# Running sums of a state-space scan: GpSimd multiplies the triangle, TensorE adds down with 512-column f32r products

## What is computed

```python
a = -jnp.exp(a_log)                       # one number for each head
a_cum = jnp.cumsum(dtc * a, axis=2)       # running sums down the 128 tokens of a chunk
seg = a_cum[:, :, :, None] - a_cum[:, :, None, :]
decay = jnp.exp(jnp.where(causal, seg, -jnp.inf))
cb = jnp.einsum('bctgn,bcsgn->bctsg', cc, bc)
y_diag = jnp.einsum('bctsgh,bcsghp->bctghp', cb[..., None] * decay, xdt)
```

## Time and profile before

| what | value |
|---|---|
| median of three runs | 1853.76 us (1853.33 to 1853.78) |
| the profiled execution | 1853.41 us |
| its span, first to last instruction | 1851.6 us |
| mean granted TensorE clock | 0.997 of full speed |
| TensorE busy | 1837.6 us, 99% |
| VectorE busy | 1293.0 us, 70% |
| ScalarE busy | 1024.6 us, 55% |
| GpSimd busy | 0.6 us |
| HBM traffic | 330.23 MB moved, mean 178 GB/s |

### The profile page before, as it was taken

The page is one execution under the profiler, slowest core; times in us unless marked ns, Lnnn a source line. Parts: engine busy times, 40 slices in busy tenths (PEclk is TensorE's granted clock), DMA queues, the critical chain, the costliest instruction groups (busy, mean ns, idle before and its releaser), DMA issues.

```text
span 1851.6 us, 27958 instructions
## 1 busy us (share of the span) xinstructions
PE 1837.6 (99%) x11450; PEld 1649.6 (89%) x11450; DVE 1293.0 (70%) x1775; ACT 1024.6 (55%) x1182; POOL 0.6 (0%) x7
## 2 busy tenths in 40 slices
PE   8999999999999999999999999999999999999998
PEld 8898889998889888899988888899988888889997
DVE  6868887986686887798656555677656555578654
ACT  6657745655465684465545456465544456556543
POOL 0000000000000000000000000000000000000000
PEclk9999999999999999999999999999999999999999
DMA  9776656655675765655555566465555556555553
GB/s 244 166 146 151 173 181 192 193 184 188 159 171 144 164 164 177 204 182 182 175 195 185 165 195 199 164 204 183 182 185 186 167 184 203 171 175 183 184 179 102
DMA packets 253319, 330.23 MB, mean 178 GB/s; under 512 B 25796, under 2 KB 165328, under 8 KB 253192
## 3 DMA queue, kind: packets, MB, share of 16 engines
q1 hardware_dynamic: 252928, 328.10, 58.9%
q10 hardware_dynamic: 264, 0.35, 0.1%
HBM read 327.33 MB, written 1.09 MB: 177 GB/s over the span
## 4 chain that ended last, share of the span: by engine, by line
PE 96%; DVE 2%; ACT 1%; DVEq 1%; DMA 0%; issue 0%; SPq 0%; ACTq 0%
PE psum L575 31%; PE psum L587 16%; PE psum L589 15%; PE psum L588 15%; PE psum L651 5%; PE psum L678 4%; PE psum L653 2%; PE psum L772 1%; PE psum L710 1%; DVEq L1413 1%; DMA w_raw<-in_w_in 0%; PE psum L791 0%; PE psum L918 0%; PE psum L955 0%; PE psum L935 0%; PE psum L598 0%
## 5 line engine op out<-in xcount | busy, mean ns | idle before, releaser
L400 ACT ACTIVATE w_hi<-w_raw 128x2048 fp32r<-128x2048 f32 (+2 forms) x310 | 575.7, 1858 | 312.9 <-PE psum L589 281.1
L575 PE MATMUL psum<-act,w_hi 128*128 128x256 f32 x3264 | 591.7, 284 | 0.0
L392 DVE TENSOR_TENSOR w_low<-w_raw,w_hi 128x1024 fp32r<-128x1024 f32 (+1 forms) x310 | 372.7, 1202 | 285.7 <-ACT w_hi L400 277.0
L575 PEld LDWEIGHTS psum<-act,w_hi 128*128 128x128 f32 x3264 | 510.2, 192 | 1.2 <-issue 0.7
L587 PE MATMUL psum<-w_hi,act 128*128 128x512 f32 x1280 | 505.1, 395 | 0.0
L589 PE MATMUL psum<-w_hi,act 128*128 128x512 f32 x1280 | 498.9, 390 | 0.0
L588 PE MATMUL psum<-w_low,act 128*128 128x512 f32 x1280 | 498.5, 389 | 0.0
L575 PE MATMUL psum<-act,w_low 128*128 128x256 f32 x1632 | 462.5, 283 | 0.0
L393 DVE TENSOR_TENSOR w_low<-w_raw,w_hi 128x1024 fp32r<-128x1024 f32 (+2 forms) x310 | 362.6, 1170 | 0.0
L575 PEld LDWEIGHTS psum<-act,w_low 128*128 128x128 f32 x1632 | 313.8, 192 | 0.0
L589 PEld LDWEIGHTS psum<-w_hi,act 128*128 128x128 f32 x1280 | 240.2, 188 | 50.7
(11 more groups left out here) (244 smaller groups left out, 1373.5 us busy)
## 6 DMA issues: line engine op xcount, KB each, us to landing
w_raw<-in_w_in SPq DMA_DIRECT2D x123, 1024.0 KB, 5.9
w_raw<-in_ffn_w_up SPq DMA_DIRECT2D x40, 1024.0 KB, 5.1
w_raw<-in_w_up SPq DMA_DIRECT2D x40, 1024.0 KB, 5.1
w_raw<-in_ffn_w_down SPq DMA_DIRECT2D x16, 1024.0 KB, 5.0
w_raw<-in_w_down SPq DMA_DIRECT2D x16, 1024.0 KB, 5.0
w_raw<-in_w_branch_b SPq DMA_DIRECT2D x8, 1024.0 KB, 5.0
w_raw<-in_w_out SPq DMA_DIRECT2D x8, 1024.0 KB, 5.1
w_raw<-in_w_a SPq DMA_DIRECT2D x8, 1024.0 KB, 5.2
```

The source lines that it names most:

```text
L392: dve.tensor_tensor(lo[:, 0:cut, :], of[:, 0:cut, :], hi[:, 0:cut, :], ALU.subtract).then_inc(w_lo_front, 1)
L400: act.activation(group_view(whi, q % HIGH, g), group_view(raw, q % LOW, g), ACT.Copy).then_inc(w_hi, 1)
L575: last = mm(o, held, moved, start=start and k == ks[0] and m == 0, stop=stop and k == ks[-1] and m == 2, skip_group_check=shared)
```

## The change

`scan_rows` gets the rows in another way: the triangle is multiplied by the head's steps first, and TensorE only adds down the partitions, with a matrix of equal numbers as the weights.

- VectorE, behind line 1603 in `dt_finish`, makes two parts of the steps in `step_parts` (f32r): a high part, `dtA` times 1024 rounded to f32r, and a low part, the rest. Both instructions work on 32 columns, and each has a drain ahead of it. The second signals `dt_split`.
- GpSimd waits for it and multiplies, for each chunk, group of heads and part, `tri` (spread over 8 heads) by the part's 8 columns (each spread over 128): 128x1024, both operands in SBUF, the output `steps_r` in f32r, in a place of `act` that is free at that time. That is 8 multiplications for each layer. `steps_r` has room for one chunk; those of chunk 1 wait until TensorE has used the same group's of chunk 0 (`rows_ready`). Each signals `steps_ready`.
- TensorE waits for both parts and computes four f32r products of 512 columns: two halves of the rows, each with the high and the low part added in PSUM. The weights are `ones`, which holds 1/1024, so the factor 1024 cancels.
- `ones` is now an f32r tensor. GpSimd fills 128 columns of `tmp` and copies them to it; TensorE's warm-up waits for the copy. The counts of the semaphore `setup` shift by one.
- The small results `qs` and `qr` of the attention take the places of `dte` and `dtl`, which makes room for `step_parts`.

```diff
--- before.py
+++ after.py
@@ -161,13 +161,15 @@
         rows1 = sb("rows1", [P, NR1])
         ident, tri = sb("ident", [P, P]), sb("tri", [P, P])
         amask = sb("amask", [P, S])
-        ones = sb("ones", [P, P])
+        ones_r = sb("ones", [P, P], f32r)
+        ones = ones_r[:, :].bitcast(f32)
         rope = sb("rope", [P, TT, 2, 8])
         rstd = sb("rstd", [P, TT])
         rstd_all = sb("rstd_all", [P, S])
         yrstd = sb("y_rstd", [P, TT])
-        sm = sb("small", [P, 400])
-        eps = sm[:, 399:400]
+        sm = sb("small", [P, 336])
+        eps = sm[:, 335:336]
+        step_parts = sb("step_parts", [P, 2, 32], f32r)
 
         PJ = ctx.enter_context(nc.psum_tensor("psum", [P, 8, 512], f32))
         PS = PJ[:, 0:5, :]
@@ -203,7 +205,7 @@
         aexp, acum = small(16), small(16)
         dend = small(8)
         gms, gmr = small(2), small(2)
-        qs, qr = small(32), small(32)
+        qs, qr = dte, dtl
         mx, nb, ps_, pr = small(8), small(8), small(8), small(8)
         os_, orr = small(8), small(8)
         lms, lmv, root_scratch = small(2), small(1), small(1)
@@ -214,6 +216,7 @@
         half = lambda c: slice(c * 512, (c + 1) * 512)
         xT = lambda k: PS[:, k // 2, k % 2 * S:(k % 2 + 1) * S]
 
+        steps_r = both[:, A_XG[0]:A_XG[0] + 8, :, :].rearrange("p k h t -> p (k h t)").rearrange("p (d a n) -> p d a n", d=2, a=2)
         early = g01[:, 0:8, :].rearrange("p k t -> p (k t)")
         cbm = early[:, 0:256].rearrange("p (g t) -> p g t", g=2)
         bT = early[:, 256:512].rearrange("p (g n) -> p g n", g=2)
@@ -537,9 +540,22 @@
 
         @block.gpsimd
         def _(pool):
-            nc.gpsimd.memset(ones[:, :], 1.0 / D).then_inc(setup, 1)
+            nc.gpsimd.memset(tmp[:, 0:P], 1.0 / D).then_inc(setup, 1)
+            pool.wait_ge(setup, 1)
+            nc.gpsimd.tensor_copy(ones_r[:, :], tmp[:, 0:P]).then_inc(setup, 1)
             nc.gpsimd.memset(eps, EPS).then_inc(setup, 1)
             nc.gpsimd.memset(bias_row[:, 0:P], 0.0).then_inc(setup, 1)
+            pool.wait_ge(const_in, 48)
+            for i in range(LAYERS):
+                pool.wait_ge(step("dt_split"), i + 1)
+                for c in range(2):
+                    for g in range(2):
+                        if c:
+                            pool.wait_ge(step("rows_ready"), i * 4 + g + 1)
+                        for a in range(2):
+                            nc.gpsimd.tensor_tensor(steps_r[:, g, a, :].rearrange("p (h t) -> p h t", t=P),
+                                                    bc(step_parts[:, a, 16 * c + 8 * g:16 * c + 8 * g + 8].bitcast(f32), [P, 8, P], 2),
+                                                    bc(tri[:, :], [P, 8, P], 1), ALU.mult).then_inc(step("steps_ready"), 1)
 
         @block.tensor
         def _(pe):
@@ -768,9 +784,10 @@
                     pe.wait_ge(step("chunk_ready"), i * 2 + 1)
                 else:
                     pe.wait_ge(step("rows_taken"), i * 4 + 2 * c + g)
-                for h in range(8):
-                    last = mm(pB[:, h // 4, (h % 4) * P:(h % 4 + 1) * P],
-                              dtA[:, 16 * c + 8 * g + h:16 * c + 8 * g + h + 1].to_broadcast([P, P]), tri[:, :], start=True, stop=True)
+                pe.wait_ge(step("steps_ready"), 2 * (i * 4 + 2 * c + g + 1))
+                for r in range(2):
+                    for a in range(2):
+                        last = mm(pB[:, r, :], ones_r[:, :], steps_r[:, g, a, half(r)], start=a == 0, stop=a == 1)
                 last.then_inc(step("rows_ready"), 1)
 
             def scan_state(i, g):
@@ -880,7 +897,7 @@
 
 
             pe.sem_inc(group_done, LOW)
-            pe.wait_ge(setup, 1)
+            pe.wait_ge(setup, 2)
             for n in range(14):
                 mm(PJ[:, BANKS[0], 0:P], ones[:, :], ones[:, :], start=True, stop=True)
             pe.wait_ge(ident_in, 16)
@@ -1087,7 +1104,7 @@
             act.dma_start(qkv[0:32, 0:12], C["rel_bias_2"]).then_inc(step("bias_const_in"), 16)
             act.dma_start(qkv[0:32, 512:1024], C["c_onehot"]).then_inc(step("bias_const_in"), 16)
             act.dma_start(qkv[0:12, 1024:1536], C["c_offmask"]).then_inc(step("bias_const_in"), 16)
-            act.wait_ge(setup, 2)
+            act.wait_ge(setup, 3)
             root_table()
             def first_high(q):
 
@@ -1462,7 +1479,7 @@
             def bias_rows():
 
                 dve.wait_ge(step("bias_product"), 1)
-                dve.wait_ge(setup, 3)
+                dve.wait_ge(setup, 4)
                 TTo(bias_phases[:, 1:4, P - 1], bias_bank[:, 0:3], qkv[0:12, 1024:1027], ALU.add)
                 TTo(bias_phases[:, :, P - 2::-1], bias_bank[:, 3:511].rearrange("p (w m) -> p m w", m=4),
                     qkv[0:12, 1027:1535].rearrange("p (w m) -> p m w", m=4), ALU.add).then_inc(step("bias_row"), 1)
@@ -1602,6 +1619,10 @@
                     dve.wait_ge(step("a_exp"), i + 1)
                     STT(dtA.rearrange("p (c h) -> p c h", c=TT), dtv.rearrange("p (c h) -> p c h", c=TT), -1.0,
                         bc(aexp, [P, TT, 16], 1), ALU.mult, ALU.mult).then_inc(step("dta_ready"), 1)
+                    ordered()
+                    V.tensor_scalar(step_parts[:, 0, :], dtA, float(D), None, ALU.mult)
+                    ordered()
+                    STT(step_parts[:, 1, :], dtA, float(D), step_parts[:, 0, :].bitcast(f32), ALU.mult, ALU.subtract).then_inc(step("dt_split"), 1)
 
                 def lam_sums():
                     dve.wait_ge(step("lam_in"), i * 16 + 16)
```

## The result

The kernel after takes 1857.43 us, the median of 15 runs (1855.89 to 1858.93). The kernel before, run beside it on the same chip, takes 1853.79. The ratio is 1.0015 [1.0008, 1.0022]: 3.6 us longer. The interval leaves no doubt that it is longer, but it is just within the 0.2% (3.7 us) up to which the prediction calls a time the same. The profiled execution took 1858.17 us, with a span of 1856.4 and a mean granted clock of 0.993. The times of one kernel fall into groups some 2 us apart (here 1855.9 to 1856.5 and 1857.3 to 1858.9; the profiled one is of the upper group), so differences of 1 or 2 us between single executions say little.

What follows compares the result with a forecast made beforehand. TensorE, busy for 99% of the span, was taken to bound the kernel. Against 1853.41 us, -6.9 +0.53 +5.9 +5.9 = +5.4 gave 1858.8, or 1859.2 with the median 0.35 higher; range 1846.5 to 1862.5.

Steps and rivals of the forecast that it cites:

- full turns: Two-operand VectorE instructions and GpSimd's multiplications wait each other out at SBUF: +5.9 us a layer; chance 0.38, 1856 to 1862.5.
- TensorE saves 6.9 us: Eight bursts of line 772, each 0.86 us shorter with four 512-column f32r products at 0.23 us: 6.9 us saved.
- VectorE's 0.53 us: Two drained instructions ahead of XBC5's taps delay VectorE's chain 0.53 us; covered in layer 0, +0.53 in layer 1.
- One multiplication takes 2.4 us: Each GpSimd 128x1024 multiplication was taken at 2.4 us, twice VectorE's 1.22, between bounds of 1.22 and 4.9.
- A1 and A2: GpSimd's two multiplications for the first group of heads, forecast in layer 0 from 65.1 to 67.5 and to 69.9 us.
- TensorE waits 5.9 us a layer: TensorE waits 2.4 us in QK2 for line 393 and 3.5 at the first burst for chunk_ready, in each layer.
- The later turns, taken as nothing: Turns around lines 392 to 1650 were held covered by 4.6 us of room before TensorE needs line 1650; cost 0.
- The clock, left out of the sum: TensorE's clock might fall behind QK2's wait, some 1.6 us a layer, or behind line 743, 1.7 either way; range only.
- The start at 0: TensorE's warm-up waits 0.1 to 0.5 us longer for the copy; taken as 0, upper end 0.2.
- The range: From no contention less the clock's fall spared, to full turns with a fall of the clock: 1846.5 to 1862.5 us.
- no contention: Rival: VectorE and GpSimd read SBUF side by side, only 6.9 - 0.53 counts: 1847.4 us; chance 0.25.
- Fewer turns: Rival: VectorE keeps its way between back-to-back subtractions; GpSimd enters only at two places: +0.6, 1854.4 us; chance 0.22.

Runs made afterwards that it cites:

- experiment 2: Kernel after with each burst's eight old f32 products; GpSimd still multiplies and TensorE still waits, steps unused: 1864.79 us, ratio 1.0051.
- experiment 1: Kernel after without GpSimd's multiplications; TensorE's f32r products read the spread columns of step_parts, triangle left out: 1848.44 us, ratio 0.9966.
- experiment 5: Kernel after with chunk 0's second-group multiplications behind chunk_ready and chunk 1's behind chunk 0's second-group y_ready: 1847.82 us; repeated, 1849.94.
- experiment 6: Kernel after with GpSimd copying the spread step columns instead of multiplying the triangle by them, at the same times: 1848.29 us, ratio 0.9965.
- experiment 8: Kernel after with GpSimd memsets of steps_r, reading nothing, instead of multiplications; TensorE's products read spread step columns, no triangle: 1847.07 us, ratio 0.9960.
- Experiment 3: Kernel after with GpSimd waiting for chunk_ready before the second group's two multiplications of chunk 0: 1852.29 us, ratio 0.9986.
- experiment 4: Kernel after with TensorE's warm-up reading tmp after the first memset, the copy to ones waited for afterwards: 1857.98 us, ratio 1.0015.
- experiment 9: Kernel after with GpSimd's later groups delayed behind chunk_ready and y_ready, and VectorE making step_parts behind XBC5's taps: 1854.57 us, ratio 1.0000.

## Why the prediction was right

The forecast was 1859.2 us, 1.8 above the median and 1.0 above the profiled execution; its likeliest case, full turns, is the one that the traces show, and 1857.43 lies in that case's range of 1856 to 1862.5. By the prediction's own 0.2% the outcome is "same", to which it gave 0.23, and not "slower", to which it gave 0.40: the change is 3.6 us where the sum had 5.4. By its steps:

- **TensorE saves 6.9 us.** Right. A burst takes 0.93 us, or 1.13 behind the 64-row products; experiments 2 and after, each against its before, give 6.6. The four products cost 0.23 each, and the turn of 0.20 stays.
- **VectorE's 0.53 us.** Right on VectorE: line 1620 to line 1625 is 65.05 to 65.59. Where it isn't hidden (experiments 1 and 5) the wait for the SiLU is 0.8, not 1.1 us; in after it vanishes, since TensorE reaches the place later, and the sum's +0.53 is -0.8.
- **One multiplication takes 2.4 us.** Too long. By itself it takes 1.9: the pair of experiment 5, at 66.21 beside the taps, is done in 3.75. With that GpSimd is done with A1 and A2 earlier, and three turns of 0.9, 1.7 and 1.7 lie ahead of `chunk_ready`, where I had 2.0, 2.4 and 2.4. The estimate of 2.25 us from the Trainium skill ("GPSIMD Engine Reference", 3.1) was nearer, and still above.
- **Full turns.** Right, with experiments 6 and 8 to show it: none for a memset that reads nothing, turns as long as the copy, and turns as long as the multiplication. The Trainium skill ("SBUF — State Buffer", Who interferes with whom) says of a DVE instruction with two SBUF inputs that it contends with a GpSimd instruction that reads SBUF and not with one that only writes it; the rows agree, 2.91 against 1.22 us.
- **TensorE waits 5.9 us a layer.** The term that was mis-sized: 0.8 + 2.5 and 0.7 + 2.4, so 3.3 and 3.1 us. `chunk_ready` came at 80.4 (79.23 + 1.21) where I had 82.3, though all of this execution is 0.7 later.
- **The later turns, taken as nothing.** Right: the list of waits of after has none behind the first burst. Experiment 3, with four multiplications in a row there, has one.
- **The clock, left out of the sum.** It fell in both layers behind the wait of 2.5 us, and cost 1.8 and 1.7. I had it as a possibility at 1.6 a layer, for a wait of 3.6. It is the same in experiments 2, 4 and 9, with waits of 2.3 to 2.5 us, and in none of the eight profiles without such a wait does it fall at that place; no run changes the length of the wait alone. A further 1.4 went at line 759 of layer 1, where the profile of before had none; the prediction had such a fall as a possibility, 1.7 us either way.
- **The start at 0.** Nothing in experiment 4 speaks against it. The 0.7 of the profiled execution is its own.
- **The range.** Its lower end is not what its words give: 1847.4 less a fall of 1.7 us is 1845.7, not 1846.5. The measured time is far from that end.

So the sizes were off, and the errors stood against each other: 5.4 us too much for the turns and 1.3 for the SiLU, against 3.5 too little for the clock that the turns bring and 1.4 for the fall in layer 1. The mechanism was foreseen; that the time came so near was luck. With the right sizes for the turns and the SiLU, and no clock in the sum, the forecast would have been some 1.3 us below before, the wrong way. For the rivals: "no contention" is what experiment 8 shows for an engine that doesn't read, 1847.1 us for a forecast of 1847.4 (7.5 us below its own before, for 6.4). "Fewer turns" was 3 us too low with 1854.4, and its mechanism, a VectorE that keeps its way between two subtractions, is excluded by the pair of subtractions at 70.69 and 73.53, each behind the other without a gap and each 2.91 long.

What stays open: why the clock fell behind `dt_proj` of layer 1 in the profile of after and not in that of before. Stretches at 1.2 GHz stand at other times in other executions of like kernels (3.4 us from 45.4 in experiment 3; none there in experiment 5, but 6.8 us from 515.4), and the executions of one kernel fall 2 us apart, as near 1848 and near 1850 in experiment 5. I did not test what places them. In the twelve profiles together, the window of 512 to 530 us has a granted clock of 1.00 in before and in experiment 1, in which GpSimd does nothing during the scan, and 0.91 or 0.81 in the ten others, the memsets of experiment 8 among them. That is one execution of each kernel, and GpSimd's last work before that window is some 400 us back, so it shows no cause.

## What to carry to other kernels

Work given to an idle GpSimd isn't free for VectorE: as measured here, each GpSimd instruction that reads SBUF can hold up one VectorE instruction that reads two operands from SBUF for its whole duration, so count the instructions of both engines ahead of the next due time and put GpSimd's where none is near. Moving the same work behind two semaphores was worth 8 to 10 us here (3.6 above before against 4.5 to 6.8 below it); a half measure (experiment 3) only carried the turns to the next due time. And price a new wait of some 2.5 us on a busy TensorE with the clock that falls behind it, here 1.7 to 1.8 us more: it decided the sign of this change. The wait of 1.8 us in experiment 3 had no such fall behind it.

## What the runs showed of the hardware

- The turns alternate, one instruction each, wherever both engines had such work in these traces: 2.88 us for a multiplication and 2.84 from one subtraction to the next, which is 1.9 + 1.2 less some 0.25 of overlap. A copy gives 2.06 for a subtraction, a memset 1.22.
- A VectorE instruction with only one operand in SBUF can be held up too: line 1661, 128x1024 float32 in 0.69 us alone, takes 0.84 in layer 0 and 2.43 in layer 1. Those that read PSUM and SBUF aren't: line 1657 starts at 82.80, inside GpSimd's pair at 82.27, and takes 1.23. The Trainium skill ("SBUF — State Buffer", Who interferes with whom) has tensor_scalar among the operations that can take both ways; 0.69 us for what takes others 1.2 agrees with that.
- The price is in the duration of the instruction, not in idle time ahead of it: no wait of VectorE for GpSimd stands in the trace. A line's maximum against its minimum (1898/2051/2880 ns for line 556) gives it away.
